# A hybrid decoder layer with 32 experts: the last expert group is served last, and the final sum of the other tokens moves beside its rounds

## The reference, cut to what matters

```
g_idx = argmax(x @ w_rg + b_rg)                   # one of 4 groups for each token
top_v, top_i = top_k(softmax(le[g_idx]), 2)       # two of the 8 experts of that group
hh = silu(x @ wg) * (x @ wu) * comb               # each expert: 1024 -> 256
y  = sum over the two experts of hh @ wd          # 256 -> 1024
out = rmsnorm(x + y, final_g)
```

## Time and profile before

| | before |
|---|---|
| median of 3 runs | 761.57 us (759.4 to 763.84) |
| the profiled execution itself | 761.19 us |
| its span | 759.4 us |
| PE busy | 705.4 us (93%) |
| DVE, ACT, POOL busy | 397.6, 213.3, 195.2 us |
| bytes moved by DMA | 173.56 MB |

### The profile page before, as it was taken

One profiled execution on the slowest core, in us unless ns is written; L12 is line 12 of the kernel. 1 busy time (PEld: TensorE's weight loads), 2 busy tenths in 40 slices (PEclk: granted clock), 3 DMA queues, 4 the chain that ended last, 5 costly groups with the idle time before them and its releaser, 6 DMA issues.

```text
span 759.4 us, 11121 instructions
## 1 busy us (share of the span) xinstructions
PE 705.4 (93%) x4071; PEld 346.7 (46%) x4071; DVE 397.6 (52%) x1107; ACT 213.3 (28%) x502; POOL 195.2 (26%) x208
## 2 busy tenths in 40 slices
PE   9999999999999999899999958999999999968575
PEld 6555555557666655455555542223222322212131
DVE  0777667774667664676565661343332333221358
ACT  3566645611551543311112110110111011100123
POOL 1011111010212423021111233755444544400111
PEclk9999999999999999999999958999999999999878
DMA  8911030040110013985221758899999999999897
GB/s 315 353 41 66 28 127 1 3 171 1 63 63 0 1 55 120 387 288 211 83 84 64 308 190 314 333 366 369 358 382 420 428 423 425 426 424 423 356 382 287
DMA packets 35544, 173.56 MB, mean 229 GB/s; under 512 B 6882, under 2 KB 13486, under 8 KB 25226
## 3 DMA queue, kind: packets, MB, share of 16 engines
q1 hardware_dynamic: 27058, 154.27, 51.6%
q0 software_dynamic: 8000, 17.24, 6.0%
q10 hardware_dynamic: 432, 1.34, 0.4%
HBM read 154.27 MB, written 25.78 MB: 237 GB/s over the span
## 4 chain that ended last, share of the span: by engine, by line
PE 65%; DVE 14%; DMA 9%; ACT 5%; issue 4%; SPq 1%; POOL 1%; DVEq 0%; POOLq 0%; ACTq 0%
PE PS L2190 17%; PE PS L2206 8%; PE PS L2009 6%; PE PS L2001 6%; PE PS L1987 4%; PE PS L1837 4%; DMA BIG<-in_wexp 4%; PE PS L1968 3%; DMA RD<-xtab,rot 2%; PE PS L1838 2%; PE PS L1957 2%; DVE RD L1225 2%; DMA BIG<-ypair 2%; PE PS L1821 2%; PE PS L2049 2%
## 5 line engine op out<-in xcount | busy, mean ns | idle before, releaser
L2190 PE MATMUL PS<-BIG,RD 128*32 128x512 f32 x1184 | 155.6, 619 | 10.7 <-issue 8.0
L881 POOL DMA_INDIRECT RD<-xtab,rot x84 | 85.2, 1014 | 39.1 <-issue 24.7
L2190 PEld LDWEIGHTS PS<-BIG,RD 128*32 128x32 f32 x1184 | 42.6, 114 | 98.7 <-issue 98.7
L2206 PE MATMUL PS<-BIG,RD 128*32 128x512 f32 x616 | 76.0, 592 | 2.2 <-issue 1.3
L1837 PE MATMUL PS<-BIG 128*128 128x512 f32 x128 | 66.1, 598 | 0.0
L1689 DVE SCALAR_TENSOR_TENSOR RD<-RD,PS 128x256 f32<-128x256 f32 x22 | 9.2, 416 | 103.4 <-ACT RD L1145 103.4
L778 POOL TENSOR_TENSOR stat<-stat,mhalf 128x1 f32<-128x1 f32 (+1 forms) x27 | 15.5, 577 | 185.3 <-DVE stat L1215 83.7
L2009 PE MATMUL PS<-BIG 128*128 128x512 f32 x128 | 59.5, 609 | 0.3 <-DVE xin L1488 0.3
L1711 DVE STREAM_TRANSPOSE RD<-RD 128x1024 f32<-128x1024 f32 x21 | 43.3, 2064 | 31.3 <-DMA RD<-xtab,rot 31.3
L2001 PE MATMUL PS<-BIG 128*128 128x512 f32 x128 | 58.2, 598 | 0.0
L1987 PE MATMUL PS<-BIG 128*128 128x344 f32 x192 | 57.3, 454 | 0.0
(11 more groups left out here) (323 smaller groups left out, 1070.8 us busy)
## 6 DMA issues: line engine op xcount, KB each, us to landing
BIG<-in_wexp SPq DMA_DIRECT2D x26, 2048.0 KB, 10.0
BIG<-in_wexp SPq DMA_DIRECT2D x30, 1024.0 KB, 16.1
RD<-in_wexp SPq DMA_DIRECT2D x4, 2048.0 KB, 17.7
BIG<-ypair SPq DMA_DIRECT2D x8, 1024.0 KB, 8.8
xin<-in_x SPq DMA_DIRECT2D x13, 512.0 KB, 4.1
BIG<-in_wxy SPq DMA_DIRECT2D x4, 1024.0 KB, 4.8
xin<-in_wexp SPq DMA_DIRECT2D x4, 1024.0 KB, 13.0
BIG<-x2d SPq DMA_DIRECT2D x1, 4096.0 KB
```

The costliest lines, as they stand in the source:

```text
L881: pool.indirect_dma_start(xg[:, p3, j * CHUNK_D:(j + 1) * CHUNK_D], None, xtab.rearrange("t (q e) -> (t q) e", q=NQ), bass.IndirectOffsetO ...
L2190: o = MM(PS[own, 2 + p2, :], xgT[:, p2, at:at + STRIP], wgu[place_of(n, j) % NG][:, k * 512:(k + 1) * 512], start=(k == 0), stop=(k == KD ...
L2206: o = MM(PS[own, 5 + half, :], hT[:, p2, k, own], wdn[place_of(n, j) % ND][:, at:at + 512], start=(k == 0), stop=(k == KF - 1))
```

## The change

The experts are put in two classes. The experts 0 to 23 come first (six with 4 strips, nine with 3, nine with 2), then the experts of group 3 (three with 3 strips, five with 2). There are again 88 strips, 22 rounds and 32 experts' weights. The strips of group 3 stand in the rounds 17 to 21 (`LATE`; round 17 has one strip of an early expert).

A new list (`clist`) gives each token a place: tokens of groups 0 to 2 fill seven tiles (0 to 6), tokens of group 3 fill two (7 and 8). More tokens in group 3 than 256, or fewer than 136, send the kernel through the general loop and the old tail, which stand now inside the branch on `nv`.

Scatters into `ypair` end with round 17 (`R_LATE`). Behind it POOL fetches, with indirect transfers, the rows of x (`tile_x`) and of the pairs (`tile_y`) for the tiles 0 to 6 into buffers of weights that are done with, and x for the tiles 7 and 8. Their sums, squares, roots and scalings are placed beside the rounds 19 to 21 and behind them. The tiles 0 to 3 are summed by DVE, the tiles 4 to 6 by PE with diagonal matrices (`dgx`). For the tiles 7 and 8 nothing goes through memory: PE multiplies the results of the late rounds with matrices `S` (`places`), which hold a token's weight where a row belongs to a place and zero elsewhere; they accumulate in four banks of PSUM over five rounds, and x is added with an identity. All tiles are stored by POOL with indirect transfers (`tile_out`).

Smaller parts: `ypair` is filled with zeros during the recurrent branch; the copies that form the scatters' index lists move from ahead of the first round into the rounds 0 and 1 (`pair_rows`); the new lists are computed in the rounds 2 and 4 and stored and read in the rounds 7 to 15. Line numbers of the changed program differ: L1711 is L1958, L1689 and L1692 are L1935 and L1938, L1705 is L1952, L2206 is L2523, L2227 is L2544, L881 is L952, L900 is L971.

The x of the late tiles, 7 and 8, is the last that POOL fetches, behind 14 other transfers. The diff, cut to what the prediction speaks of:

```diff
-NFIX, NBIG, NSMALL = 6, 12, 14
-CAPS = [4] * NFIX + [3] * NBIG + [2] * NSMALL
+NFIX, NBIG, NSMALL = 6, 9, 9
+NEARLY = NFIX + NBIG + NSMALL
+LBIG = 3
+CAPS = [4] * NFIX + [3] * NBIG + [2] * NSMALL + [3] * LBIG + [2] * (NE - NEARLY - LBIG)
...
+R_LATE = sum(CAPS[0:NEARLY]) // PER_R
+LATE = range(R_LATE, NU)
+NET, NLT = 7, 2
+NTL = NET + NLT
+SERVED = [0, 1, 2, 7, 8, 3, 4, 5, 6]
+ON_PE = [7, 8, 4, 5, 6]
...
+        tkx = [xg[:, 0, :]] + [wgu[s][:, 2048:3072] for s in (4, 5, 6)] + [wgu[6][:, 3072:4096]]
...
+        tky = [xg[:, 1:3, :].rearrange("p a b -> p (a b)")] + [wgu[s][:, 0:2048] for s in (4, 5, 6)] + [wdn[4]]
...
+        ynew = {19: wgu[0][:, 3072:4096], 20: wgu[1][:, 3072:4096], 21: wgu[3][:, 0:1024]}
+        t_banks = {7: (0, 1), 8: (7, 2), 4: (3, 4), 5: (5, 6), 6: (0, 1)}
...
-            sp.wait_ge(gu_ps, last_round(NE - 6) + 1)
-            sp.wait_ge(y_ps, 2 * last_round(NE - 5) + 2)
-            sp.dma_start(x2_all[:, 0:NPT, :], x2d[0:SEQ, :].rearrange("(t p) d -> p t d", p=P)).then_inc(x2_in, 16)
-            sp.dma_start(x2_all[0:NDEC, NPT, :], x2d[SEQ:TOKENS, :]).then_inc(x2_in, 16)
...
-            for t in range(5):
-                load_y(t)
-            for t in range(NT):
-                if t + 5 < NT:
-                    load_y(t + 5)
-                sp.wait_ge(ob_ok, t + 1)
-                rows = rows_of(t)
-                sp.dma_start(a["y"][t * P:t * P + rows, :], ob[0:rows, t % NO, :]).then_inc(o_out[t % NO], 16)
...
+            pool.wait_ge(mem0, 8)
+            pool.dma_start(ypair[0:TOPK * SEQ, :].rearrange("(p n) d -> p n d", p=P),
+                           zeros.rearrange("p (o d) -> p o d", o=1).to_broadcast([P, TOPK * NPT, D_MODEL])).then_inc(lists_init, 16)
+            pool.dma_start(ypair[TOPK * SEQ:, :], zeros[0:TOPK * NDEC]).then_inc(lists_init, 16)
...
+            def tile_x(k):
+                alone(pool)
+                pool.indirect_dma_start(tkx[k], None, x2d, token_of(k), bounds_check=TOKENS - 1, oob_is_err=False)\
+                    .then_inc(tile_in[min(k, NET)], 16)
+            def tile_y(k):
+                alone(pool)
+                pool.indirect_dma_start(tky[k], None, ypair.rearrange("(q two) d -> q (two d)", two=2), token_of(k),
+                                        bounds_check=TOKENS - 1, oob_is_err=False).then_inc(tile_in[k], 16)
+            def tile_out(k):
+                pool.wait_ge(ob_ok, SERVED.index(k) + 1 + OB_OK)
+                alone(pool)
+                pool.indirect_dma_start(a["y"], token_of(k), oL[k - NET] if k >= NET else tkx[k], None,
+                                        bounds_check=TOKENS - 1, oob_is_err=False).then_inc(y_out, 16)
...
+            for n in range(1, R_LATE + 1):
                 if n + 4 < NU:
                     gather(n + 4)
+                if n == R_BIG:
+                    pool.wait_ge(pid_ok, 3)
                 spread_round(n)
...
+            pool.wait_ge(xgd_ok, NU)
+            tile_x(0)
+            pool.wait_ge(gu_ps, last_round(25) + 1)
+            tile_x(1)
+            for p in range(2):
+                pool.wait_ge(yo_out[p], 16 * ((R_LATE + 2 - p) // 2))
+            tile_y(0)
+            tile_y(1)
+            pool.wait_ge(gu_ps, last_round(27) + 1)
+            tile_x(2)
+            tile_y(2)
+            tile_x(3)
+            tile_y(3)
+            pool.wait_ge(y_ps, 2 * last_round(25) + 2)
+            tile_x(4)
+            tile_y(4)
+            pool.wait_ge(gu_ps, last_round(29) + 1)
+            tile_x(5)
+            tile_y(5)
+            tile_x(6)
+            tile_y(6)
+            pool.wait_ge(y_ps, 2 * last_round(27) + 2)
+            tile_x(7)
+            tile_x(8)
+            tile_root(0)
+            tile_root(1)
+            tile_out(0)
...
+            def square(k):
+                act.wait_ge(ss3_ok, SERVED.index(k) + 1)
+                if k not in ON_PE:
+                    act.wait_ge(x3_ok, k + 1 + X3_OK)
+                    A(junk[:, :], tkx[k], ACT.Square, accum_out=ss3[:, k:k + 1]).then_inc(ss3_ok, 1)
+                    return
+                act.wait_ge(x3p_ps, ON_PE.index(k) + 1 + X3P_PS)
+                lo, hi = t_banks[k]
+                A(junk[:, 0:HALF], PS[:, lo, :], ACT.Square, accum_out=ss3[:, k:k + 1])
+                A(junk[:, HALF:], PS[:, hi, :], ACT.Square, accum_out=ss3b[:, k:k + 1]).then_inc(ss3_ok, 1)
 
...
+            def places(i):
+                V.tensor_scalar(S[i], iota, qw[:, i, 0:1], qw[:, i, 1:2], ALU.is_equal, ALU.mult).then_inc(S_ok, 1)
+            def tile_add(k):
+                x = tkx[k]
+                dve.wait_ge(tile_in[k], 32 + TILE_IN[k])
+                V.scalar_tensor_tensor(x, tky[k][:, 0:D_MODEL], cl[:, k, 1:2], x, ALU.mult, ALU.add).then_inc(dve_done, dq.up())
+                dve.wait_ge(dve_done, dq.now())
+                V.scalar_tensor_tensor(x, tky[k][:, D_MODEL:], cl[:, k, 2:3], x, ALU.mult, ALU.add).then_inc(x3_ok, 1)
...
+            def tile_finish(k):
+                dve.wait_ge(rs3_ok, SERVED.index(k) + 1 + RS3_OK)
+                r3 = rs3[:, k:k + 1]
+                if k not in ON_PE:
+                    V.scalar_tensor_tensor(tkx[k], tkx[k], r3, gfb, ALU.mult, ALU.mult).then_inc(ob_ok, 1)
+                    return
+                out = oL[k - NET] if k >= NET else tkx[k]
+                lo, hi = t_banks[k]
+                V.scalar_tensor_tensor(out[:, 0:HALF], PS[:, lo, :], r3, gfb[:, 0:HALF], ALU.mult, ALU.mult)
+                V.scalar_tensor_tensor(out[:, HALF:], PS[:, hi, :], r3, gfb[:, HALF:], ALU.mult, ALU.mult).then_inc(ob_ok, 1)
 
...
+                if n < 2:
+                    pair_rows((2 * n, 2 * n + 1))
...
+                if n == 18:
+                    dve.wait_ge(gu_ps, last_round(25) + 1)
+                    dve.wait_ge(qw_in, 16 * len(LATE) + QW_IN)
+                    dve.wait_ge(cl_in, 32 + CL_IN)
+                    for i in range(4):
+                        places(i)
+                if n == 19:
+                    dve.wait_ge(gu_ps, last_round(26) + 1)
+                    places(4)
+                    for i in range(3):
+                        for k in range(TOPK):
+                            o = V.tensor_scalar(dgx[:, i, k, :], ident, cl[:, 4 + i, 1 + k:2 + k], None, ALU.mult)
+                    o.then_inc(dgx_ok, 1)
+                    tile_add(0)
+                    tile_add(1)
+                if n == 20:
+                    tile_add(2)
+                    tile_total(0)
+                    tile_total(1)
+            tile_finish(0)
+            tile_finish(1)
+            tile_add(3)
+            for i in range(2, NTL):
+                tile_total(SERVED[i])
+                if i >= 3:
+                    tile_finish(SERVED[i - 1])
+            tile_finish(SERVED[NTL - 1])
...
+            def late_chunk(i, c):
+                j, half = divmod(c, 2)
+                return MM(PS[:, t_banks[NET + j][half], :], S[i][:, j * P:(j + 1) * P],
+                          yo_of(LATE[i])[:, 512 * half:512 * half + 512], start=(i == 0), stop=(i == len(LATE) - 1))
+            def late_rows(i, chunks, built):
+                pe.wait_ge(S_ok, built + S_OK)
+                pe.wait_ge(yoa_ok, LATE[i] + 2)
+                pe.wait_ge(yod_ok, LATE[i] + 2)
+                for c in range(chunks):
+                    o = late_chunk(i, c)
+                    if i == len(LATE) - 1 and c % 2:
+                        o.then_inc(x3p_ps, 1)
...
+                if n == 19:
+                    late_rows(0, 3, 4)
+                    late_rows(1, 3, 4)
+                if n == 20:
+                    late_rows(2, 3, 5)
+                    for i in range(3):
+                        late_chunk(i, 3)
...
+            late_rows(3, 4, 5)
+            pe.wait_ge(tile_in[NET], 32 + TILE_IN[NET])
+            for j in range(NLT):
+                for half in range(2):
+                    MM(PS[:, t_banks[NET + j][half], :], ident, tkx[NET + j][:, 512 * half:512 * half + 512], start=False, stop=False)
+            late_rows(4, 4, 5)
+            pe.wait_ge(dgx_ok, 1 + DGX_OK)
+            for k in ON_PE[NLT:]:
+                pe.wait_ge(tile_in[k], 32 + TILE_IN[k])
+                if k == 6:
+                    pe.wait_ge(ob_ok, SERVED.index(NET) + 1 + OB_OK)
+                for half in range(2):
+                    out, own = PS[:, t_banks[k][half], :], slice(512 * half, 512 * half + 512)
+                    MM(out, ident, tkx[k][:, own], start=True, stop=False)
+                    MM(out, dgx[:, k - 4, 0, :], tky[k][:, own], start=False, stop=False)
+                    o = MM(out, dgx[:, k - 4, 1, :], tky[k][:, D_MODEL + 512 * half:D_MODEL + 512 * half + 512], start=False, stop=True)
+                o.then_inc(x3p_ps, 1)
...
+    order = order - (np.arange(NE) >= NEARLY) * (1 << 20)
```

383 lines of the change are left out of this document (284 added, 99 removed).

## The result

The change makes the kernel slower: 777.0 us median (774.8 to 779.9) against 762.7 us for the kernel before on the same chip, ratio 1.0193, 95% interval 1.0157 to 1.0228. The profiled execution took 775.12 us with a span of 773.4 us. Forecast were 765 us, range 755 to 771: the result lies outside.

What follows compares the result with a forecast made beforehand. DMA bytes behind 560 us and PE's order behind 663 us were taken as bounds. Late x at 732.5 us, 22.2 us of products to 754.7, then the tail gave span 763.0, execution 765 us, range 755 to 771.

Steps and rivals of the forecast that it cites:

- Lists and zeros: cost 0: New list work in the rounds and zero filling in the recurrent branch fit into pauses of DVE and POOL; 0 us.
- fallback: If a gather came late in rounds 7 to 9, up to 0.5 us in each of three rounds.
- the sum for x of the late tiles: DMA bytes packed to 729.4 us, plus 2 us edge and 1.1 us index copies: tiles 7 and 8 land at 732.5.
- Bytes and rate: Behind round 17, 4.62 MB more on full engines at 424 GB/s, 10.9 us; at the skill's 358 GB/s, 12.9 us.
- Index copies: Twelve copies before round 2's hidden rows put 1.3 us on PE's path; 1.1 us kept, range 0 to 1.4.
- Zeros: 8.45 MB behind 161 us, 20 us of DMA and 16 us of POOL, fit in a wait; 0 us, otherwise 0 to 3.
- PE before the last down product: Round 20's gate and up start near 688.5 us, then 36.2 us of work; last down product taken to end at 728.
- The sign of DVE's waits on tiles: Near the last rounds, no wait of DVE on a tile (L2001) is longer than PE's work beside it.
- Behind PE: After PE's last product at 754.7 us: squares, sum, two scalings to 759.0, then stores; end near 763.0 us.
- (a): Tile transfers share engines with the last weights; last down product ends behind 729 us, execution 769 (766 to 774); chance 0.21.
- (b): Extra bytes find room before 560 us through earlier releases, PE alone counts; execution 757.4 (752 to 760); chance 0.22.
- (c): Counts over a limit send the kernel into the general loop and old tail; above 810 us; chance 0.01.

Runs made afterwards that it cites:

- e4: Changed kernel without the table of places and class rows, so no tile rows are fetched or stored; ratio to the kernel before 1.0057.
- e13: Kernel before with only the new order of the experts (tail, scatters and queue rule as before); ratio 0.9986.
- e16: Changed kernel with weights queue sorted by need, class rows two per round in rounds 5 to 9, table write in round 5, index copies before round 0; ratio 1.0132.
- e15: Kernel before plus 16-byte rows only: nine indirect transfers to scattered places in rounds 7 to 9 and a table write in round 7; ratio 1.0007.
- e18: Changed kernel with the class rows placed 64 bytes apart; ratio to the kernel before 1.0258, with no run of the changed kernel on that chip.
- e1: Changed kernel without the table of places (ACT's two writes and POOL's five gathers left out); ratio to the kernel before 1.0144.
- e3: Changed kernel with class rows and the table's write two rounds earlier (rounds 5 to 7 and 5); ratio to the kernel before 1.0156.
- e17: Kernel before plus nine indirect transfers of 16-byte rows, written to neighbouring places, and the table's write; ratio 1.0115.
- e2: Changed kernel with class-row transfers one in each of rounds 7 to 15 instead of three in rounds 7 to 9; ratio to the kernel before 1.0129.

## Why the prediction was wrong, step by step

**The step that failed is "Lists and zeros: cost 0", in its half on the lists.** It counted POOL's issues (10.5 of 10.8 us in a round) and looked at no engine of the DMA, though the windows had these full from 560 us on and the rounds 7 to 9 begin there. From 560 to 680 us after moves 403 GB/s instead of 424: 2.5 MB, at 424 GB/s 5.9 us (e4, without the lists, 421). Its fallback (a late gather, 0.5 us in three rounds) had the kind right, with stops of 1.91 and 0.20 us before turnings, but not the main effect: the weights behind the lists land later. Both late places follow. Down of round 18 starts 123.1 us behind round 10's gate and up, against 118.1 in e13 with the same order: 5.0 of the 8.3 us. The other 3.3 us lie ahead of round 10, where 0.9 us are the index copies and executions vary by the rest (round 3's gate and up starts at 490.3 us in before, at 487.9 in e13). And the sum for x of the late tiles, 732.5 us, is 738.4 us with 5.9 added; measured 740.06, so that 1.7 us have no owner. That the lists cost the time is shown by the rates; that the engines lose it in the other queues' packets, too. Why a short row does that to them is open.

**Bytes and rate.** Right as far as it can be told. 4.62 MB more and 424 GB/s made 732.5 us, and e16, whose lists lose less behind 560 us, lands x at 733.3 us, but in an execution whose rounds run 3 us earlier than before's, which helps it. The 358 GB/s of the Trainium skill (DMA: Bandwidth & Descriptors, Specifications) does not bound this kernel: the trace has 43 us at 424.

**Index copies.** Right in mechanism, too large. The twelve copies took 1.04 us instead of 1.3, and PE's stop behind them grew from 0.43 us to 1.29, by 0.9 us (forecast 1.1 to 1.3):

```profile
490.50 0.44 PE L2544 MATMUL PS<-cst,RD 128*128 128x128 f32 x2 [1.29 <-DVE RD L1938]
```

**Zeros.** Right: POOL's next work in that branch (L889) starts at 199.96 us (199.71 before). The issue takes 1.2 us where 16 were estimated from the gathers' price; this plain transfer wasn't charged by the row.

**PE before the last down product.** Undersized. The order's share was put at 3.1 us (688.5 for 685.4); counted from round 10 it is 5.9 us in e13, and 688.9 us came out there because that execution ran 2.4 us ahead. With the lists on top the start came to 696.2. From there 37.2 us instead of 36.2: PE stops 1.56 us before round 21's turning, since DVE is busy with the sums of two tiles, which stand ahead of the hidden rows in its order. The sign of DVE's waits on tiles held (0.51 us here, and 8.67 us for the tile before, beside which PE worked on), but the order of DVE's work stopped PE:

```profile
720.78 1.28 DVE L2001 SCALAR_TENSOR_TENSOR BIG<-BIG,wr 128x1024 f32<-128x1024 f32 x1 [0.51 <-DMA BIG<-ypair,wr]
722.10 1.28 DVE L2003 SCALAR_TENSOR_TENSOR BIG<-BIG,wr 128x1024 f32<-128x1024 f32 x1
723.30 0.41 DVE L1935 SCALAR_TENSOR_TENSOR RD<-RD,PS 128x256 f32<-128x256 f32 x1
724.23 0.44 PE L2544 MATMUL PS<-cst,RD 128*128 128x128 f32 x2 [1.56 <-DVE RD L1938]
```

**Behind PE.** The 26 products took 22.5 us (22.2). The tail took 10.8 us instead of 8.3, the second term that was mis-sized. POOL's timeline at the end:

```profile
766.61 1.03 POOL L1007 DMA_INDIRECT out_y<-BIG,wr  x1 [1.76 <-issue]
767.95 0.96 POOL L1007 DMA_INDIRECT out_y<-BIG,wr  x1 [0.30 <-issue]
```

DVE is done with tile 5 at 765.5 us; POOL, whose last root ended at 764.9, issues the store 1.1 us later, then tile 6's, whose issue ends at 768.9, and the span ends 4.5 us after that. The sum let POOL's delay (1.1 us) and the last, small store (1.3 us for its issue) go for nothing.

**Rivals.** (a) Its sign came (last down product at 733.4, behind 729) and its time (769) was nearer than the forecast. Half of its mechanism came as well: the last weights, asked for at 687.1 us, landed 33.0 us later, at 720.1 (its sum had about 719; before 709.5), so the tiles do share the engines with them. But this did not delay the last down product: behind 690.4 us PE waits for no weights and comes to it at 729.75, and e4, without a byte of tiles, ends its last down product at 732.0. A sign that two causes share decides nothing. (b) No room appeared: 363 GB/s before 560 us, none gained. (c) Did not happen.

The misses add up: 7.6 us at the landing of x (5.9 of them the lists, by the rates), 0.3 in the 26 products, 2.5 in the tail: 763.0 + 10.4 = 773.4 us of span. This adds along the path that was last. Had x alone been on time, PE would still have come to L2614 only at 737.0 us, and 3.0 of the 7.6 us would have come back. The lists delay the weights too, and with them PE; how much of the rest goes with them no single run shows.

What stays open: which property of the 16-byte rows stops the engines. Number of packets alone (e15), three transfers in a row (e15 again) and a distance under 64 bytes (e18) are ruled out as the only cause; neighbouring places fit after, e1, e3, e16 and e17 against e15, but e17 ran on another chip, and e16, which ran on e15's, is another kernel.

## What to carry to other kernels

A transfer on full DMA engines is not priced by its bytes. Its own time goes by its packets (16 KB in rows of 16 bytes took 40 us on full engines, 8 us on those of e3), and what it costs the others has to be read from their rate (371 GB/s instead of 420). Small tables may belong in a stretch where the windows show a low DMA share (here before 450 us), or in few long rows; neither was tried. What was tried is to spread the class rows over the rounds (e2), which raised the rate. And when a sum says that bytes bound the end, every added transfer between the point where the engines fill and the end is a term of it, however small.

A theory from one trace needs its change alone on the old kernel: e4 seemed to convict the order of the experts, e13 acquitted it of the loss. And compare two executions from a common point within them, not by the clock of each: 688.9 us looked like the forecast only in an execution that ran ahead.
